# Three dead attention buffers as a landing zone for the next expert, copied to the ring by GpSimd

## The chip, the cores and the metric

One core of a Trainium2 chip runs the whole kernel. The time is device microseconds (us) of one execution, as the median of several runs. PE is TensorE, DVE is VectorE, ACT is ScalarE, POOL is GpSimd, SP is SyncE, whose only work here is to issue DMAs.

## What is computed

One transformer layer in float32 for 256 latent tokens of width 1024, with 256 context tokens: modulation rows from SiLU(c), neighbourhood attention over a 64-wide grid, a residual, and a mixture of 32 experts, four for each token.

```python
hx = modulate(x, norm_g[0], sh1, sc1)
mx = neighbourhood_attention(q, k, v, kc, vc, na_rpb) @ na_w_o
x = x + g1 * rms_norm(mx, norm_g[1])
hx2 = modulate(x, norm_g[2], sh2, sc2)
logits = hx2 @ w_router + b_router           # top 4 of 32, softmax over them: gates
for e in range(32):
    hid = hx2 @ w_up[e] + b_up[e]            # 1024 x 2048
    x_glu = minimum(hid[:, :1024], 7)
    x_lin = clip(hid[:, 1024:], -7, 7)
    act = x_glu * sigmoid(1.702 * x_glu) * (x_lin + 1)
    out = out + gates[:, e] * (act @ w_down[e] + b_down[e])    # 1024 x 1024
x = x + g2 * rms_norm(out, norm_g[3])
```

The weights of an expert are 12 MB (six chunks of 2 MB), those of all experts 403 million bytes. Each is read once.

## The kernel before

**Stages.** PE multiplies the modulation weights (`ada`), then the projections, then 16 rounds of attention (`DUOS`), the output projection (`wo`), the router, and then the blocks of experts. A block is up to 64 tokens of one expert (`SLOTS`). An expert with more than 64 tokens has two or more blocks; the tables that say which block belongs to which expert (`whose_i`, `ends_i`) are made on the chip in the first block, and `tables_ready` marks them.

**The ring.** All big weights go through `ring`, 12 places of 1 MB. In the expert stage it is six places of 2 MB, one for each chunk of an expert: chunks 0 to 3 are the up weights, 4 and 5 the down weights. So the ring holds one expert. SP loads chunk j of expert e when PE has used chunk j of the last block of expert e - 1: PE adds one to `ring_free` for each chunk of each block, SP waits for the count that the tables give, and the DMA adds to `expert_in[j]`. All these loads go through one DMA queue in the order of issue. PE waits for `expert_in[j]` ahead of chunk j (`expert_chunk_here`).

**One block on PE** (`block_step`), in the order of its queue: the up matmuls (L1201, 16 a chunk), the bias (L1211), `combine(0, b)` (L1187), transposes for the gates (L1223), the gather of the next block's tokens (L1127), `combine(1, b)` (L1187), which needs the accumulation of the first half (`acc_done`), the transposes of the activation (L1233, L1237), which need `act_ready`, the transposes of the next tokens (L1135), and the down matmuls (L1248).

**The same block on DVE**, in its queue: `glu` (L905) and `lin` (L906) from PSUM, `act = (lin + 1) * glu` (L909, both inputs in SBUF), `add_part(0)` (L899, twice, PSUM and SBUF), `act * sig` (L915, both inputs in SBUF, gives `act_ready`), `bsel` (L860), `aT` (L918), `add_part(1)` (L899), and the selection matrices for the next block (L854, L848). ACT makes the sigmoid (L579) and four copies out of PSUM.

**GpSimd** has done its last work ahead of the router (`powers(5, 1)`) and waits for `ms_ready` until the very end (`powers(6, 1)`).

**The memory** that matters: `kT_mem`, `tokens` (which also holds the attention bias) and `v_mem` are 2 MB each. After the attention `kT_mem` holds the residual `x1` and `h2T`, `tokens` the split biases of the experts (`bup_parts`, `bdown`), and `v_mem` the small tensors of the expert block (`xT`, `glu`, `lin`, `sig`, `act`, `aT`, `y`, `combT`). ACT issues the loads of `x1`, `b_up` and `b_down` when the attention ends; DVE splits `b_up` into three bfloat16 parts (`bup_split`) while PE is in the output projection.

Of the kernel before, what the change touches and what calls it, by code (L numbers as in the profile page):

```python
# [18 lines left out]
BF16 = mybir.dt.bfloat16  # L19
# [23 lines left out]
PER, UPS = 6, 4  # L43
# [3 lines left out]
def build(nc, x, c, ctx_in, c_ctx, ada_w, ada_b, norm_g, w_qkv, w_o, rpb, w_router, b_router,  # L47
          w_up, b_up, w_down, b_down, out):
    with ExitStack() as st:
# [9 lines left out]
        def sem(name):  # L59
# [8 lines left out]
        tokens = sb("tokens", [P, 4, D])  # L68
        bias = tokens[:, :, :].rearrange("p a d -> p (a d)")[:, 0:BIAS_SLOTS * BIAS_ROWS * GRID_W].rearrange(
            "p (b c) -> p b c", c=BIAS_ROWS * GRID_W)  # L70
# [6 lines left out]
        kT_mem = sb("kT_mem", [P, KC * 512])  # L77
        kT = kT_mem[:, :].rearrange("p (k t) -> p k t", k=KC)
        x1 = kT_mem[:, 0:2048].rearrange("p (t d) -> p t d", t=2)
        h2T = kT_mem[:, 2048:4096].rearrange("p (k t) -> p k t", k=KC)  # L80
# [3 lines left out]
        v_mem = sb("v_mem", [P, 4 * D])  # L84
        v = v_mem[:, :].rearrange("p (t d) -> p t d", t=4)

        xT = v_mem[:, 0:512].rearrange("p (j s) -> p j s", j=4)
        glu = v_mem[:, 512:1024]
        lin = v_mem[:, 1024:1536]
        sig = v_mem[:, 1536:2048]  # L90
        act = v_mem[:, 2048:2560]
        aT = v_mem[:, 2560:3072].rearrange("p (j s) -> p j s", j=4)
        y = v_mem[:, 3072:3584]
        combT = v_mem[:, 3584:3840].rearrange("p (t s) -> p t s", t=2)
        tmp = v_mem[:, 0:2048].rearrange("p (t d) -> p t d", t=2)
        junk = v_mem[:, 2048:3072]
# [4 lines left out]
        gate1, shift2, scale2, gate2 = mod  # L101

# [6 lines left out]
        adab = sb("adab", [P, 3, HALF])  # L109
        rows = sb("rows", [P, HALF])  # L110
# [34 lines left out]
        bup = tokens[0:E, 0:2, :].rearrange("p a d -> p (a d)")  # L145
        xe = hT_mem[:, 0:HALF]
        bup_parts = tokens[:, 2, :].bitcast(BF16)[0:3 * E, :]
        bup_part = hT_mem[0:E, 2048:3072].bitcast(BF16)
        bdown = tokens[0:E, 3, :]
# [8 lines left out]
        block_no = sb("block_no", [E, NCOL])  # L158
        whose_i = sb("whose_i", [1, NCOL], I32)
# [28 lines left out]
        wo_done, x1_ready, h2_ready = sem("wo_done"), sem("x1_ready"), sem("h2_ready")  # L188
        h2T_done, h2T_ready, logit_done = sem("h2T_done"), sem("h2T_ready"), sem("logit_done")
# [22 lines left out]
        def expert_chunk_here(eng, e, j):  # L212

            eng.wait_ge(expert_in[j], e * 16 + 16)
# [64 lines left out]
        def _(sp):  # L279
# [53 lines left out]
            def expert(e, blocks_before):  # L333
# [5 lines left out]
            for j in range(PER):  # L339
# [3 lines left out]
            with sp.Fori(1, E) as e:  # L343
                blocks_before = sp.value_load(ends_i[0:1, bass.ds(e - 1, 1)], min_val=1, max_val=E + MAX_EXTRA)
# [8 lines left out]
        def _(pool):  # L353
# [92 lines left out]
            for k in range(2, 6):  # L446
                powers(k, 1)
# [835 lines left out]
```

## Time and profile before

| | us |
|---|---|
| median of 3 runs | 1288.15 (1287.13 to 1288.61) |
| the profiled execution, its own time | 1288.93 |
| its span, first to last instruction | 1287.2 |
| PE busy | 1207.2 (94%) |
| DVE, ACT, POOL busy | 372.5, 185.8, 59.2 |
| chain that ended last: PE, DMA | 52%, 39% of the span |
| mean granted TensorE clock | 0.985 |

The span lacks 1.7 us of the execution's own time: what lies before the first and after the last instruction. The DMA engines moved 454 MB, 353 GB/s over the span. The stage of experts runs from 276.9 to the end and has 35 blocks (L905, which runs once a block, is counted 35 times): 32 experts, three of them with two blocks. A block in which nothing waits takes 27.3 us. "U" below is the time at which the first up matmul of a block starts.

### The profile page before, as it was taken

The numbers are of one execution on the slowest core, as the hardware profiler recorded it, in microseconds if no ns is written. First come the engines' busy times: TensorE is split into PE (matmuls) and PEld (weight loads), VectorE is DVE, ScalarE is ACT, GpSimd is POOL, SyncE is SP. The second block draws the span as 40 slices with busy tenths as digits, with TensorE's granted clock in tenths as the row PEclk, the third lists the DMA queues.
The fourth block names the chain that finished last, engine by engine and source line by source line (L and its number), as shares of the span: only waits on it lengthen the run. The fifth ranks groups of instructions, "written<-read, shape, count | busy, mean of one in ns | idle before, by whom it ended". The sixth has DMA issues, their size and how long they took to land.

```text
span 1287.2 us, 15187 instructions
## 1 busy us (share of the span) xinstructions
PE 1207.2 (94%) x5850; PEld 536.9 (42%) x5851; DVE 372.5 (29%) x737; ACT 185.8 (14%) x360; POOL 59.2 (5%) x89
## 2 busy tenths in 40 slices
PE   5899999889999999999999999999999999999996
PEld 1888655453343433333333333333443333333342
DVE  1944364631321112222111111122211122211114
ACT  2200264110111001110010000011110011101001
POOL 2230053000000000000000000000000000000000
PEclk9899999979999999999999999999999999999998
DMA  9973488309499999999999999999699999999590
GB/s 372 369 208 131 160 258 318 130 27 383 184 415 429 430 428 429 427 429 430 428 429 427 429 430 428 429 428 403 256 416 429 429 427 429 428 428 429 238 391 33
DMA packets 49044, 454.40 MB, mean 353 GB/s; under 512 B 16736, under 2 KB 16776, under 8 KB 20320
## 3 DMA queue, kind: packets, MB, share of 16 engines
q1 hardware_dynamic: 48064, 450.90, 84.7%
q0 software_dynamic: 512, 1.72, 0.4%
q10 hardware_dynamic: 448, 1.50, 0.4%
q8 instruction: 13, 0.21, 0.1%
q14 instruction: 7, 0.06, 0.0%
HBM read 453.06 MB, written 1.05 MB: 353 GB/s over the span
## 4 chain that ended last, share of the span: by engine, by line
PE 52%; DMA 39%; DVE 4%; issue 2%; ACT 1%; SPq 0%; POOL 0%; DVEq 0%; POOLq 0%
DMA ring<-in_moe_w_up 37%; PE pair L1201 23%; PE pair L1248 9%; PE pair L1010 9%; PE pair L1091 2%; DMA ring<-in_ada_w 2%; PE pair L1187 1%; PE pair L1026 1%; PE pair L968 1%; DVE hT_mem L899 1%; PE pair L1036 1%; PE pair L1049 1%; DVE v_mem L905 1%; DVE v_mem L906 1%; PE pair L1135 1%
## 5 line engine op out<-in xcount | busy, mean ns | idle before, releaser
L1201 PE MATMUL pair<-ring,v_mem 128*64 128x512 f32 x2240 | 495.8, 594 | 29.6 <-DMA ring<-in_moe_w_up 29.2
L1201 PEld LDWEIGHTS pair<-ring,v_mem 128*64 128x64 f32 x2240 | 181.1, 137 | 336.0 <-issue 274.5
L1248 PE MATMUL pair<-ring,v_mem 128*64 128x512 f32 x1120 | 248.1, 595 | 1.5
L905 DVE TENSOR_SCALAR v_mem<-pair 128x512 f32<-128x512 f32 x35 | 24.2, 692 | 719.8 <-PE pair L1211 719.8
L1248 PEld LDWEIGHTS pair<-ring,v_mem 128*64 128x64 f32 x1120 | 92.5, 137 | 132.9 <-issue 132.7
L579 ACT ACTIVATE v_mem<-v_mem 128x512 f32<-128x512 f32 x35 | 22.1, 630 | 538.8 <-DVE v_mem L905 538.8
L899 DVE TENSOR_TENSOR hT_mem<-hT_mem,pair 128x512 f32<-128x512 f32 x140 | 89.4, 680 | 8.0 <-PE pair L1187 8.0
L1187 PE MATMUL pair<-v_mem 64*128 64x512 f32 x280 | 78.8, 641 | 3.4 <-ACT v_mem L591 0.8
L1127 PE MATMUL pair<-q_mem,pT_mem 128*64 128x512 f32 x288 | 71.5, 618 | 1.3 <-DVE pT_mem L848 1.3
L379 POOL TENSOR_TENSOR rstd<-ms,neghalf 128x1 f32<-128x1 f32 (+1 forms) x8 | 4.7, 594 | 1071.7 <-DVE ms L627 1071.7
L591 ACT ACTIVATE v_mem<-pair 128x512 f32<-128x512 f32 x35 | 20.9, 597 | 228.7 <-PE pair L1248 228.7
L1010 PE MATMUL pair<-mod_high,ring_low 128*128 128x256 f32 (+1 forms) x128 | 44.7, 349 | 4.7 <-DVE ring_low L691 4.6
L1187 PEld LDWEIGHTS pair<-v_mem 64*128 64x128 f32 x280 | 21.2, 185 | 48.7 <-DVE hT_mem L899 32.6
L968 PE MATMUL pair<-ring,condT 128*32 128x512 f32 x192 | 25.7, 663 | 9.4 <-DMA ring<-in_ada_w 9.4
L564 ACT ACTIVATE hT_mem<-pair 128x512 f32<-128x512 f32 x36 | 21.5, 597 | 77.7 <-PE pair L1127 77.7
L1127 PEld LDWEIGHTS pair<-q_mem,pT_mem 128*64 128x64 f32 x288 | 17.8, 138 | 28.5 <-issue 27.1
L1010 PEld LDWEIGHTS pair<-mod_high,ring_low 128*128 128x128 f32 x128 | 25.4, 198 | 8.2 <-DVE ring_low L691 5.7
L1091 PE MATMUL pair<-ring,hT_mem 128*128 128x512 f32 x64 | 27.7, 594 | 0.0
L909 DVE SCALAR_TENSOR_TENSOR v_mem<-v_mem 128x512 f32<-128x512 f32 x35 | 24.2, 692 | 3.7
L918 DVE COPY v_mem<-pair 128x256 f32<-128x256 f32 x35 | 14.9, 424 | 35.1 <-PE pair L1233 35.1
L1010 PE MATMUL pair<-ring_low,mod_high 128*128 128x512 f32 x64 | 24.9, 389 | 0.0
L915 DVE TENSOR_TENSOR v_mem<-v_mem 128x512 f32<-128x512 f32 x35 | 24.0, 686 | 0.0
(217 smaller groups left out, 944.5 us busy)
## 6 DMA issues: line engine op xcount, KB each, us to landing
ring<-in_moe_w_up SPq DMA_DIRECT2D x128, 2048.0 KB, 23.2
ring<-in_moe_w_down SPq DMA_DIRECT2D x64, 2048.0 KB, 20.3
ring<-in_ada_w SPq DMA_DIRECT2D x24, 1024.0 KB, 8.4
ring<-in_na_w_qkv SPq DMA_DIRECT2D x12, 1024.0 KB, 27.4
ring<-in_na_w_o SPq DMA_DIRECT2D x4, 1024.0 KB, 15.1
tokens<-in_na_rpb SPq DMA_DIRECT2D x32, 96.0 KB, 6.4
gain<-in_norm_g POOLq DMA_DIRECT2D x3, 512.0 KB, 5.7
tokens<-in_x SPq DMA_DIRECT2D x1, 1024.0 KB, 5.0
```

What stands on the lines that cost most here:

```text
L579: s.activation(sig, glu, ACT.Sigmoid, scale=ALPHA).then_inc(sig_ready, 1)
L899: d.tensor_tensor(dst, dst, bank[banks[n]][:, :], ALU.add).then_inc(acc_done, 1)
L905: d.tensor_scalar(glu, bank[0][:, :], LIMIT, None, ALU.min).then_inc(glu_ready, 1)
L909: d.scalar_tensor_tensor(act, lin, 1.0, glu, ALU.add, ALU.mult).then_inc(pre_ready, 1)
L915: d.tensor_tensor(act, act, sig, ALU.mult).then_inc(act_ready, 1)
L968: last = mm(bank[b][32 * j:32 * j + 32, :], condT[:, k, :], wchunk(n)[:, HALF * j:HALF * j + HALF], start=k == 0, stop=k == KC - 1)
L1010: last = mm(out_, left, right, start=k == 0 and part == 0, stop=k == KC - 1 and part == 2)
L1091: last = mm(bank[4 + 2 * t + i][:, :], oT[:, k, P * t:P * t + P], wpair(WO, k)[:, HALF * i:HALF * i + HALF], start=k == 0, stop=k == KC - 1)
L1127: last = mm(bank[3][64 * n:64 * n + 64, :], pick[:, t, :], h2[:, t, HALF * n:HALF * n + HALF], start=t == 0, stop=t == 1)
L1187: mm(bank[banks[n]][:, :], combT[64 * n:64 * n + 64, t, :], y[64 * n:64 * n + 64, :], start=True, stop=True).then_inc(part_done, 1)
L1201: last = mm(bank[half][64 * n:64 * n + 64, :], xT[:, k % 4, 64 * (k // 4):64 * (k // 4) + 64], w[:, c0:c0 + HALF], start=k == 0, stop=False)
L1248: last = mm(bank[2][64 * n:64 * n + 64, :], aT[:, j, 64 * half:64 * half + 64], w[:, HALF * n:HALF * n + HALF], start=k == 0, stop=k == KC ...
```

## The change

The three 2 MB buffers become one tensor `zone`, and its three parts are the landing places of chunks 0, 1 and 2 of the next expert. SP loads them there (`staged_chunk`), and GpSimd copies each to its place in the ring (`g.tensor_copy`, 128 x 4096 float32) when the chunk has landed and the last block of the expert before has used that place. A tiny GpSimd operation on `home_mark` stands ahead of each copy. PE waits for the copy (`staged[j]`) in place of the landing for chunks 0 to 2. Chunks 3, 4 and 5 go straight to the ring as before.

The order of SP's queue becomes: chunks 0 to 3 of expert 0; chunks 0, 1, 2 of expert 1 into the zone as the attention gives its parts free (`s_done`, `bias_used`, `o_done`); chunks 4 and 5 of expert 0; then for each expert e from 1 on: chunks 3, 4, 5 of e, and behind them chunks 0, 1, 2 of e + 1 into the zone, each when the copy of the same chunk of e is done.

What was in the three buffers moves: the block's small tensors to `hT_mem` and two `mod` buffers (`glu` and `xe` share one place, `lin` and `act` another), `x1` to a buffer shared with `adab` and `rows`, `h2T` to `hT_mem`, the biases to `hT_mem`, `gain` and `mod[0]`. So the loads of `b_up` and `x1` are issued later, `b_down` behind the residual, `gate2` is made ahead of the split of `b_up`, ACT's squares wait for the split (`bup_split`), and `take_xe` waits for `pre_ready` and `sig_ready`.

```diff
-PER, UPS = 6, 4
+PER, UPS, STAGED = 6, 4, 3
+ZONE = 6
...
+        zone = sb("zone", [P, ZONE, 2048])
+        kT_mem = zone[:, 0:2, :].rearrange("p s n -> p (s n)")
+        token_mem = zone[:, 2:4, :].rearrange("p s n -> p (s n)")
+        v_mem = zone[:, 4:6, :].rearrange("p s n -> p (s n)")
...
+        v = v_mem.rearrange("p (t d) -> p t d", t=4)
+        tmp = acc
+        last_tmp = v_mem[:, 0:2048].rearrange("p (t d) -> p t d", t=2)
+        last_junk = v_mem[:, 2048:3072]
...
+        xT = hT_mem[:, 0:512].rearrange("p (j s) -> p j s", j=4)
+        glu, xe = hT_mem[:, 512:1024], hT_mem[:, 512:1024]
+        lin, act = hT_mem[:, 1024:1536], hT_mem[:, 1024:1536]
+        sig = hT_mem[:, 1536:2048]
+        aT = mod[2][:, 0:512].rearrange("p (j s) -> p j s", j=4)
+        y = mod[2][:, 512:1024]
+        combT = mod[1][:, 704:960].rearrange("p (t s) -> p t s", t=2)
...
+        row_mem = sb("row_mem", [P, 2 * D])
+        adab = row_mem[:, 0:3 * HALF].rearrange("p (g n) -> p g n", g=3)
+        rows = row_mem[:, 3 * HALF:4 * HALF]
+        x1 = row_mem[:, :].rearrange("p (t d) -> p t d", t=2)
...
+        junk = pT_mem[:, :]
+        bup = hT_mem[0:E, 2048:4096]
+        bup_parts = gain[:, :].bitcast(BF16)[0:3 * E, :]
+        bup_part = pT_mem[0:E, :].bitcast(BF16)
+        bdown = mod[0][0:E, :]
...
         def expert_chunk_here(eng, e, j):
-            eng.wait_ge(expert_in[j], e * 16 + 16)
+            if j < STAGED:
+                eng.wait_ge(staged[j], e + 1)
+            else:
+                eng.wait_ge(expert_in[j], e * 16 + 16)
+
+        def staged_chunk(j):
+
+            return zone[:, 2 * j:2 * j + 2, :].rearrange("p s n -> p (s n)")
...
-            def load_expert(e, j):
+            def load_expert(e, j, dst):
                 src = (up_2k[bass.ds(e, 1), j] if j < UPS else down_4k[bass.ds(e, 1), j - UPS])
-                sp.dma_start(expert_chunk(j), src.rearrange("a p n -> (a p) n")).then_inc(expert_in[j], 16)
-
...
+                sp.dma_start(dst, src.rearrange("a p n -> (a p) n")).then_inc(expert_in[j], 16)
+
+            for j in range(4):
+                sp.wait_ge(ring_free, EXP - RING + 2 * j + 2)
+                load_expert(0, j, expert_chunk(j))
+            sp.wait_ge(s_done, DUOS)
+            sp.wait_ge(expert_in[0], 16)
+            load_expert(1, 0, staged_chunk(0))
+            sp.wait_ge(bias_used, DUOS)
+            sp.wait_ge(expert_in[1], 16)
+            load_expert(1, 1, staged_chunk(1))
+            sp.wait_ge(o_done, DUOS)
+            sp.wait_ge(expert_in[2], 16)
+            load_expert(1, 2, staged_chunk(2))
+            for j in range(4, PER):
+                sp.wait_ge(ring_free, EXP - RING + 2 * j + 2)
+                load_expert(0, j, expert_chunk(j))
+
+            def second_half(e):
+
+                blocks_before = sp.value_load(ends_i[0:1, bass.ds(e - 1, 1)], min_val=1, max_val=E + MAX_EXTRA)
+                for j in range(STAGED, PER):
                     sp.wait_ge(ring_free, blocks_before * PER + (EXP - PER + j + 1))
-                    load_expert(e, j)
-
-            for j in range(PER):
-                sp.wait_ge(ring_free, EXP - RING + 2 * j + 2)
-                load_expert(0, j)
+                    load_expert(e, j, expert_chunk(j))
+
...
-                expert(e, blocks_before)
+            with sp.Fori(1, E - 1) as e:
+                second_half(e)
+                for j in range(STAGED):
+                    sp.wait_ge(staged[j], e + 1)
+                    load_expert(e + 1, j, staged_chunk(j))
+            second_half(E - 1)
             for t in range(2):
                 sp.wait_ge(fin_ready, t + 1)
-                sp.dma_start(out[0][P * t:P * t + P, :], tmp[:, t, :]).then_inc(out_done, 16)
+                sp.dma_start(out[0][P * t:P * t + P, :], last_tmp[:, t, :]).then_inc(out_done, 16)
...
+            for j in range(STAGED):
+                pool.wait_ge(expert_in[j], 16)
+                g.memset(staged_mark[:, j:j + 1], 0.0).then_inc(staged[j], 1)
+                g.memset(home_mark[:, j:j + 1], 0.0).then_inc(home_free[j], 1)
+            pool.wait_ge(tables_ready, 1)
+            with pool.Fori(1, E) as e:
+                blocks_before = pool.value_load(ends_i[0:1, bass.ds(e - 1, 1)], min_val=1, max_val=E + MAX_EXTRA)
+                for j in range(STAGED):
+                    pool.wait_ge(expert_in[j], e * 16 + 16)
+                    pool.wait_ge(staged[j], e)
+                    pool.wait_ge(home_free[j], e)
+                    pool.wait_ge(ring_free, blocks_before * PER + (EXP - PER + j + 1))
+                    mark = staged_mark[:, j:j + 1]
+                    g.tensor_tensor(home_mark[:, j:j + 1], mark, mark, ALU.add).then_inc(home_free[j], 1)
+                    g.tensor_copy(expert_chunk(j), staged_chunk(j)).then_inc(staged[j], 1)
...
-            sc.wait_ge(s_done, DUOS)
+            sc.wait_ge(o_done, DUOS)
+            sc.dma_start(bup, b_up[0]).then_inc(in_bup, 16)
+            sc.wait_ge(bc_done, 8)
             sc.dma_start(x1, token_rows(x)).then_inc(in_res, 16)
-            sc.wait_ge(bias_used, DUOS)
-            sc.dma_start(bup, b_up[0]).then_inc(in_bup, 16)
-            sc.dma_start(bdown, b_down[0]).then_inc(in_bdown, 16)
+            sc.wait_ge(bup_split, 1)
...
                 sc.wait_ge(x1_ready, t + 1)
+                if t == 1:
+                    sc.dma_start(bdown, b_down[0]).then_inc(in_bdown, 16)
                 sc.wait_ge(ssq_ready, 6 + 3 * t)
                 s.activation(junk, x1[:, t, :], ACT.Square, accum_out=ssq3[:, t:t + 1]).then_inc(ssq_ready, 1)
...
                 sc.wait_ge(gather_done, b + 1)
+                if not isinstance(b, int) or b > 0:
+                    sc.wait_ge(pre_ready, b)
+                    sc.wait_ge(sig_ready, b)
                 s.activation(xe, bank[3][:, :], ACT.Copy).then_inc(xe_ready, 1)
...
+            ve.wait_ge(in_gain, 48)
+            for i in range(2):
+                ve.wait_ge(bc_done, 6 + i + 1)
+                h = slice(HALF * i, HALF * i + HALF)
+                d.tensor_tensor(gate2[:, h], bank[2 + i][:, :], gain[:, h], ALU.mult).then_inc(bc_dve, 1)
+            ve.wait_ge(bc_dve, 6)
             ve.wait_ge(in_bup, 16)
...
             d.tensor_copy(bup_parts[2 * E:3 * E, :], bup).then_inc(bup_split, 1)
-            ve.wait_ge(in_gain, 48)
-            for i in range(2):
-                ve.wait_ge(bc_done, 6 + i + 1)
-                h = slice(HALF * i, HALF * i + HALF)
-                d.tensor_tensor(gate2[:, h], bank[2 + i][:, :], gain[:, h], ALU.mult).then_inc(bc_dve, 1)
...
-                d.tensor_tensor(tmp[:, t, :], acc[:, t, :], gate2[:, :], ALU.mult).then_inc(gated, 1)
+                d.tensor_tensor(last_tmp[:, t, :], acc[:, t, :], gate2[:, :], ALU.mult).then_inc(gated, 1)
```

## Rows read from the trace of the kernel before

**Rows 1.** The page, second part: busy tenths of the 16 DMA engines in 40 slices of 32.2 us.

```profile
DMA  9973488309499999999999999999699999999590
```

**Rows 2.** Chain that ended last, in order of time: start us, us, what.

```profile
471.36 13.75 PE pair L1201 x64
...
509.76 3.68 PE pair L1201 x16
513.59 25.48 DMA ring<-in_moe_w_up
539.12 3.68 PE pair L1201 x16
...
891.50 3.65 PE pair L1201 x16
...
1045.21 13.75 PE pair L1201 x64
...
1201.06 3.65 PE pair L1201 x16
```

**Rows 3.** The chain and the timeline of one block, 334.87 to 362.17: start us, us.

```profile
334.87 13.73 PE pair L1201 x64
...
362.17 13.73 PE pair L1201 x64
...
350.47 0.69 DVE L909 SCALAR_TENSOR_TENSOR v_mem<-v_mem 128x512 f32<-128x512 f32 x1
...
351.08 1.28 DVE L899 TENSOR_TENSOR hT_mem<-hT_mem,pair 128x512 f32<-128x512 f32 x2
...
352.27 0.69 DVE L915 TENSOR_TENSOR v_mem<-v_mem 128x512 f32<-128x512 f32 x1
...
353.47 0.51 PE L1233 MATMUL pair<-ident,v_mem 128*128 128x128 f32 x2
```

**Rows 4.** Timeline of SP's issues of expert loads: start us, us, count.

```profile
304.31 3.77 SPq L331 DMA_DIRECT2D ring<-in_moe_w_down  x2
...
338.48 10.63 SPq L331 DMA_DIRECT2D ring<-in_moe_w_up  x4
...
358.90 3.77 SPq L331 DMA_DIRECT2D ring<-in_moe_w_down  x2
...
912.33 10.63 SPq L331 DMA_DIRECT2D ring<-in_moe_w_up  x4
```

**Rows 5.** DMA issues begun in 338 to 340, and in 365 to 367: KB, us to landing.

```profile
ring<-in_moe_w_up SPq DMA_DIRECT2D x1, 2048.0 KB, 7.6
...
ring<-in_moe_w_up SPq DMA_DIRECT2D x1, 2048.0 KB, 11.8
```

**Rows 6.** GpSimd groups by line: busy us, mean ns of one, idle before.

```profile
L440 POOL TENSOR_SCALAR mod<-mod,rinv 128x512 f32<-128x512 f32 x32 | 21.7, 691 | 38.1 <-DVE rinv L749 38.1
L429 POOL TENSOR_TENSOR tokens<-tokens,wmask 128x384 f32<-128x384 f32 x16 | 18.3, 1145 | 12.0 <-DMA tokens<-in_na_rpb 12.0
...
L400 POOL TENSOR_SCALAR qcol<-qcol 128x1 f32<-128x1 f32 x1 | 0.2, 234 | 0.1
```

**Rows 7.** Timeline of GpSimd and of VectorE, 55 to 64.

```profile
55.37 1.67 POOL L413 TENSOR_TENSOR hT_low<-hT_mem,mod_high 128x512 fp32r<-128x512 f32 x1 [1.50 <-DVE mod_high L678]
...
55.93 2.20 DVE L691 TENSOR_TENSOR ring_low<-ring,pT_high 128x1024 fp32r<-128x1024 f32 x1
...
62.08 1.23 DVE L691 TENSOR_TENSOR ring_low<-ring,pT_high 128x1024 fp32r<-128x1024 f32 x1
```

**Rows 8.** PE timeline with the gap before; a stretch: length, five busy times, PEclk.

```profile
21.59 1.43 PE L968 MATMUL pair<-ring,condT 128*32 128x512 f32 x8 [2.95 <-DMA ring<-in_ada_w]
...
22.50:23.00 0.50, 0.50 (x5) 0.05 (x1) 0.50 (x2) 0.00 (x0) 0.50 (x1) 0.50 0.87 361
```

**Rows 9.** Timeline of ACT's issue before the router, and of DVE in the first block.

```profile
221.34 0.44 ACTq L534 DMA_DIRECT2D tokens<-in_moe_b_down  x1
...
294.67 0.69 DVE L909 SCALAR_TENSOR_TENSOR v_mem<-v_mem 128x512 f32<-128x512 f32 x1
```

More of the change, by code:

```diff
@@ L67, in build @@
         ring = sb("ring", [P, RING, 2048])
-        tokens = sb("tokens", [P, 4, D])
-        bias = tokens[:, :, :].rearrange("p a d -> p (a d)")[:, 0:BIAS_SLOTS * BIAS_ROWS * GRID_W].rearrange(
-            "p (b c) -> p b c", c=BIAS_ROWS * GRID_W)
+        zone = sb("zone", [P, ZONE, 2048])
+        kT_mem = zone[:, 0:2, :].rearrange("p s n -> p (s n)")
+        token_mem = zone[:, 2:4, :].rearrange("p s n -> p (s n)")
+        v_mem = zone[:, 4:6, :].rearrange("p s n -> p (s n)")
+        tokens = token_mem.rearrange("p (a d) -> p a d", d=D)
+        bias = token_mem[:, 0:BIAS_SLOTS * BIAS_ROWS * GRID_W].rearrange("p (b c) -> p b c", c=BIAS_ROWS * GRID_W)
         hT_low_mem = also("hT_low", [P, KC * 512])
@@ L76, in build @@
         acc = hT_mem[:, 2048:4096].rearrange("p (t d) -> p t d", t=2)
[L77 to L80, printed above, removed]
+        kT = kT_mem.rearrange("p (k t) -> p k t", k=KC)
+        h2T = hT_mem[:, 0:2048].rearrange("p (k t) -> p k t", k=KC)
         q_mem = sb("q_mem", [P, KC * TOK])
@@ L144, in build @@
         br = sb("br", [P, E])
[L145 to L149, printed above, removed]
+        junk = pT_mem[:, :]
[3 more added lines that the diff above has]
+        bdown = mod[0][0:E, :]
         rank_e, gate_e2 = small[:, 0:2, :], small[:, 4:6, :]
@@ L158, in build @@
         block_no = sb("block_no", [E, NCOL])
+        staged_mark = sb("staged_mark", [1, STAGED])
+        home_mark = sb("home_mark", [1, STAGED])
         whose_i = sb("whose_i", [1, NCOL], I32)
@@ L188, in build @@
         wo_done, x1_ready, h2_ready = sem("wo_done"), sem("x1_ready"), sem("h2_ready")
+        staged = [sem(f"staged{j}") for j in range(STAGED)]
+        home_free = [sem(f"home_free{j}") for j in range(STAGED)]
         h2T_done, h2T_ready, logit_done = sem("h2T_done"), sem("h2T_ready"), sem("logit_done")
@@ L336, in expert @@
+            for j in range(4, PER):
[4 more added lines that the diff above has]
+                for j in range(STAGED, PER):
                     sp.wait_ge(ring_free, blocks_before * PER + (EXP - PER + j + 1))
-                    load_expert(e, j)
-            for j in range(PER):
-                sp.wait_ge(ring_free, EXP - RING + 2 * j + 2)
-                load_expert(0, j)
+                    load_expert(e, j, expert_chunk(j))
@@ L342, in _ @@
             sp.wait_ge(tables_ready, 1)
-            with sp.Fori(1, E) as e:
-                blocks_before = sp.value_load(ends_i[0:1, bass.ds(e - 1, 1)], min_val=1, max_val=E + MAX_EXTRA)
-                expert(e, blocks_before)
+            with sp.Fori(1, E - 1) as e:
[4 more added lines that the diff above has]
+            second_half(E - 1)
             for t in range(2):
@@ L600, in _ @@
                 sc.wait_ge(ssq_ready, 10 + t)
-                s.activation(junk, acc[:, t, :], ACT.Square,
+                s.activation(last_junk, acc[:, t, :], ACT.Square,
                              accum_out=ssq4[:, t:t + 1]).then_inc(ssq_ready, 1)
@@ L936, in _ @@
                 ve.wait_ge(rstd_ready, 7 + t)
-                d.scalar_tensor_tensor(tmp[:, t, :], tmp[:, t, :], rstd[:, 6 + t, 0:1], x1[:, t, :],
+                d.scalar_tensor_tensor(last_tmp[:, t, :], last_tmp[:, t, :], rstd[:, 6 + t, 0:1], x1[:, t, :],
                                        ALU.mult, ALU.add).then_inc(fin_ready, 1)
```

15 lines of the change are left out of this document (removed).

## The prediction

> **What bounds the kernel now.** I read the page first. Its busy shares name PE, but the 16 DMA engines [rows 1] stand at nine tenths or more from slice 12 on, save in slices 29 and 38 (6 and 5 tenths), and at 4 in slice 11. So no share decides: the two take turns. The chain in order of time [rows 2] shows the turns. Five blocks end with an up stage of 13.75 us without a wait (the last starts at 471.36); then each block waits 25.5 us for a landing and does only its last chunk (16 matmuls) behind it. Those ends are 29.36 us apart (509.76, 539.12): the time in which the queue moves six chunks, 4.89 us each. PE alone needs 27.30 us a block [rows 3], so it loses 2.06 us a block here. The first such stretch has 14 blocks, 485 to 895: without waits its last up stage would end at 471.36 + 14 x 27.30 + 13.73 = 867.3, and it ends at 891.50 + 3.65 = 895.15, 27.9 us lost. The second has five: 1045.21 + 5 x 27.30 + 13.73 = 1195.4 against 1204.7, 9.3 us. Together **37.1 us**, all that better supply could give in this stage.
>
> What separates the stretches are the three experts with two blocks. SP's issues [rows 4] show the first: after 304.31 nothing is issued until 338.48, for the ring is full and its places come free only in the second block (U = 334.87). The others end at 912.33 and near 1222. After each the queue is empty.
>
> **Does the zone bring supply?** In a block without waits SP issues chunk 4 at U - 3.3, chunk 5 at U, the next chunks 0 to 3 at U + 3.6 to U + 13.9 [rows 3, 4]. In the full queue only order counts, and the order of chunks is the same after the change: 3, 4, 5 of an expert, then 0, 1, 2 of the next, since SP puts the zone loads behind chunk 5. Three chunks land earlier during a double block, but chunk 3 still waits for the last use of its place, as before, so the queue runs dry there again, and the stream that sets the next stretch starts with chunk 4 at the same place (U - 3.3) as before. I see no gain. The five early chunks of the start are lost the same way: the first double is expert 1.
>
> **The copy's own price.** No row has a GpSimd copy. One-input TENSOR_SCALAR takes 0.234 us for one element a partition and 0.691 for 512 [rows 6]: 0.894 ns an element, 3.9 us for 4096. A plain copy has no scalar to read; I take 3.8. Bounds: eight times the 512 row, 5.5; the rate of the two-input row L429 (1.145 us for 384), 12.2. Below, no row excludes less. The operation on `home_mark` is 0.25 by the one-element row. Where PE waits for the stream, it now restarts at the copy of chunk 2: that landing is 4.89 earlier than that of chunk 3, plus 0.25 + 3.8 + 0.1, plus two chunks of 3.43, against 3.65 for the one chunk: 6.1 - 3.65 = 2.5 us later, paid once in each of the two stretches: 5 us, if nothing else happens.
>
> The Trainium skill (GPSIMD Engine Reference, Performance versus the Vector engine) gives 1.8 cycles an element as best case, 769 ns for 512; the row here has 691 ns and disagrees. By the page's rate the copy would be 6.1 us, an estimate, and the sum that of the last rival.
>
> **The hold.** DVE's L691 (two SBUF inputs) takes 1.23 us alone, and 2.20 when GpSimd's L413 is running: it starts at 55.93, L413 ends at 57.04, and 57.04 + 1.1 is just its end [rows 7]. So DVE waits for the whole of the other's instruction; of two that wait I let the earlier go first, GpSimd too. In the block, DVE has two operations with both inputs in SBUF, L909 and L915, and both are on PE's path [rows 3]. L413 has two inputs, the copy one; the rows can't show whether the copy holds DVE too. I take it that it does.
>
> That is the rule of the Trainium skill too (SBUF — State Buffer, Who interferes with whom): the pair of ports is an exclusive lock for the whole instruction, between any GpSimd instruction that reads SBUF and a DVE one with two SBUF inputs. It speaks against this change; for two inputs the trace agrees.
>
> **Where the copies fall, one block of a one-block expert.** A chunk issued into an empty queue lands after 7.6 us [rows 5]. Chunk 4, issued at U - 3.3, lands at U + 4.3, chunk 5 at 9.2, and the next expert's chunks 0, 1, 2 at 14.1, 19.0, 23.9 (before: chunk 0 at 365.8 + 11.8, U + 15.4, with some queue left over [rows 5]). Their places are long free.
> - Copy 0 runs from 14.35 to 18.15. L909 is due at 15.6 (350.47 [rows 3], where U + 13.73 = 348.60 ends the up stage). It waits until 18.15.
> - L909 and the two L899 take 1.8: L915 is due at 19.95. Copy 1 has been there since 19.25 and holds until 23.05. L915 ends at 23.7.
> - L1233 started at U + 18.6, 0.5 after L915 could let it. It now starts at 23.75: **5.15 us later**, and all behind it on PE's queue: the down matmuls, the block's end, and through `ring_free` SP's next chunk 4.
> - Copy 2 (24.15 to 27.95) holds only DVE's selection matrices, due one block later.
> The block takes 32.45 us. That is over 29.36, so the queue has run empty when the next chunk 4 is issued, and the next block repeats it. Nothing pulls it back.
>
> How many: the copies for expert e + 1 run in the last block of e. Experts 2 to 19 give 18 such blocks, 21 to 29 give 9. In the second block of experts 1, 20 and 30 the chunks have landed long before, and the copies run from U + 3.7 to 15.7, ahead of L909. 27 x 5.15 = **+139.0**. The DMA waits vanish, since a period of 32.4 is over the queue's: **-37.1**. In the first block the copies start at 288 and sit on L909 (294.67 [rows 9]) and L915: L915 ends 3.2 later, of which 2 was spare: **+1.2**.
>
> **The rest.** ACT issues the load of `b_down` between the residual and the square that the router waits for: **+0.4**, by the issue of 0.44 [rows 9]. The later loads of `b_up` and `x1` and the split lie under the output projection (27.7 us); by my count the DVE queue is through 0.7 us before the last half is due, so a late `gain` costs up to 2 us. This goes to the range. New waits in `take_xe` end when L909 does, ahead of the gather's end; moved tensors have the same shapes: 0. What the tail loses: GpSimd has left its loop a block before.
>
> Sum: 139.0 - 37.1 + 1.2 + 0.4 = +103.5 on the profiled execution's 1288.93: 1392.4. That execution is 0.8 over the median 1288.15, so I predict **1392 us**; for this case alone 1380 to 1410 (copy 3.4 to 4.5 us).
>
> **Rivals.**
> - *The clock falls too.* PE has two idle stretches a block, 2.4 and 2.7 us, with 1.1 us of work between. Before, PE fell to 1.2 GHz after a gap of 2.95 us (PEclk 0.50 [rows 8]). If 3 us of each down stage run at half speed, 1.5 us a block: +40, 1432 us. For it: the gap is nearly as long; against: each is shorter.
> - *One hold at most.* If the copy takes under 3.1 us, L915 comes before copy 1. The hold on L909 alone brings the block to about 29.36, the DMA's rate: 27 x 2.06 - 37.1 + 1.6 = +20, 1308 us.
> - *No hold.* A one-input copy doesn't stop DVE. Then 5.0 + 0.4: 1294 us. For it: no row shows it.
> - *The slow copy.* From 4.65 us the copies queue behind each other; at 5.5, L915 ends at 26.6, 8 us late a block: +180, 1470 us and more.
> - *The other side: the lead holds.* If three staged chunks did put the queue ahead, 3 x 4.89 = 14.7 us less in the first stretch and all 9.3 in the second: -24, 1265 us. It decides when zone loads start before the queue would be empty anyway; SP's order, behind chunk 5, speaks against it.
>
> **Chances.** Two holds 0.46, with the clock 0.14, one hold 0.13, no hold 0.12, slow copy 0.08, the lead 0.04, no difference 0.03. The range runs from no hold (1293) to the clock case with some more (1450); outside lie the lead, no difference, the slow copy and a deeper fall of the clock, 0.2. A measurement of this kernel tells 0.2% (2.6 us) from no change; faster 0.04, within it 0.03, slower 0.93.
>
> **What would show it.** GpSimd's copy row with 93 copies of near 3.8 us; L909 and L915 with means well over 0.69 us; blocks 32.4 us apart from expert 2 on, without waits for DMA; doubles' second blocks at 27.3; the DMA slices near nine tenths throughout. Wrong, if L915 keeps 0.69 while a copy runs (no hold), if blocks are 29.36 apart (one hold), or if PEclk falls in the blocks.

## The result, and the profile after

| kernel | us, median | runs | from to | profiled: own time, span | TensorE clock |
|---|---|---|---|---|---|
| before, on the same chip | 1287.64 | 4 | 1287.08 to 1288.61 | | 0.985 |
| after | 1450.49 | 4 | 1449.58 to 1452.45 | 1452.45, 1450.7 | 0.917 |

The ratio is 1.127 (95% interval 1.1246 to 1.1285): slower by 163 us, where I had forecast 1392 us, and half a microsecond above the range's end. The direction and the main mechanism, two holds in each of 27 blocks, are the forecast ones. The size is 58 us off, for the most part because the forecast had no term for the TensorE clock.

In the kernel after, line numbers are higher: the up matmul L1201 is L1253, the down matmul L1248 is L1300, DVE's L909 and L915 are L961 and L967, the transposes L1233 are L1285. From the page of the kernel after, second part (granted clock, busy DMA engines, in 40 slices of 36.3 us), then groups:

```profile
PEclk9999999689988889999999999999999999999999
DMA  9863687135888888888888888888388888888831
...
L493 POOL COPY ring<-zone 128x4096 f32<-128x4096 f32 x93 | 333.7, 3588 | 0.0
L957 DVE TENSOR_SCALAR hT_mem<-pair 128x512 f32<-128x512 f32 x35 | 24.2, 692 | 681.8 <-PE pair L1263 681.8
L1300 PE MATMUL pair<-ring,mod 128*64 128x512 f32 x1120 | 291.2, 679 | 0.3
...
L492 POOL TENSOR_TENSOR home_mark<-staged_mark 1x1 f32<-1x1 f32 x93 | 17.2, 185 | 787.0 <-DMA zone<-in_moe_w_up 634.1
...
L967 DVE TENSOR_TENSOR hT_mem<-hT_mem 128x512 f32<-128x512 f32 x35 | 107.4, 3067 | 0.0
L961 DVE SCALAR_TENSOR_TENSOR hT_mem<-hT_mem 128x512 f32<-128x512 f32 x35 | 93.0, 2657 | 3.7
```

A copy takes 3.59 us (3.8 taken), its mark 0.18. L961 and L967, 0.69 us each before [rows 3], now have means of 2.7 and 3.1; L957, which reads PSUM, stays at 0.69. The DMA slices, nine tenths before [rows 1], are at eight. TensorE's waits in the kernel after (us in total, times, longest) show where that goes:

```profile
PE pair L1285 <- DVE hT_mem L967: 69.4, 27, 2.6
PE pair L1239 <- DVE hT_mem L951: 66.9, 27, 2.7
```

27 of each, in the 27 blocks that were counted, and no wait for an expert load is left: the 37.1 us of before are gone, and 136.3 us (5.05 a block) stand in their place. One such block starts at 377.71 and the next at 412.07. The timeline of the kernel after, for this block on GpSimd, DVE and TensorE, then for the first block on GpSimd and DVE (start us, us, and in brackets the idle time before):

```profile
392.11 3.59 POOL L493 COPY ring<-zone 128x4096 f32<-128x4096 f32 x1
...
397.02 3.59 POOL L493 COPY ring<-zone 128x4096 f32<-128x4096 f32 x1
...
393.31 2.94 DVE L961 SCALAR_TENSOR_TENSOR hT_mem<-hT_mem 128x512 f32<-128x512 f32 x1
...
397.37 3.79 DVE L967 TENSOR_TENSOR hT_mem<-hT_mem 128x512 f32<-128x512 f32 x1
...
397.50 1.13 PE L1239 MATMUL pair<-mod 64*128 64x512 f32 x4 [2.33 <-DVE hT_mem L951]
401.22 0.70 PE L1285 MATMUL pair<-ident,hT_mem 128*128 128x128 f32 x2 [2.59 <-DVE hT_mem L967]
...
299.21 3.59 POOL L493 COPY ring<-zone 128x4096 f32<-128x4096 f32 x1
302.77 0.18 POOL L492 TENSOR_TENSOR home_mark<-staged_mark 1x1 f32<-1x1 f32 x1
302.90 3.59 POOL L493 COPY ring<-zone 128x4096 f32<-128x4096 f32 x1
...
302.27 4.76 DVE L961 SCALAR_TENSOR_TENSOR hT_mem<-hT_mem 128x512 f32<-128x512 f32 x1
```

The first copy ends at 395.70, and L961 is through 0.55 later (396.25); the second ends at 400.61, and L967 is through at 401.16. Two holds, two gaps, 4.92 us. But the block is 34.36 long and the block without waits 27.30 [rows 3], so 2.1 us are missing. They are in the granted clock of TensorE. Stretches of the same kernel (length, then the five engines' busy times, PEclk, DMA share, GB/s):

```profile
398.00:400.00 2.00, 0.63 (x4) 0.00 (x0) 2.00 (x1) 0.39 (x1) 2.00 (x1) 1.00 1.01 434
400.00:402.00 2.00, 0.78 (x4) 0.79 (x5) 1.31 (x3) 0.00 (x0) 0.83 (x3) 0.52 1.00 426
402.00:404.00 2.00, 2.00 (x8) 1.09 (x8) 2.00 (x4) 0.98 (x2) 2.00 (x1) 0.50 1.01 434
404.00:406.00 2.00, 2.00 (x8) 0.71 (x6) 2.00 (x4) 0.00 (x0) 1.50 (x1) 0.50 0.73 311
406.00:408.00 2.00, 2.00 (x8) 0.52 (x6) 0.17 (x2) 0.00 (x0) 0.00 (x0) 0.77 0.00 0
```

After the two gaps the clock stands at 0.50 (1.2 GHz) from about 400 to 407, the down stage takes 8.87 us instead of 7.09 (8.4 to 8.7 in the later ones of the 27), and its group's mean is 679 ns where it was 595. The last row also shows the queue empty (DMA share 0.00), as forecast: the next chunk waits for the late down stage.

Two terms more are at the start. TensorE's first up matmul is at 284.55 instead of 276.94. From DVE's waits in the kernel after:

```profile
DVE mod L833 <- DMA gain<-in_norm_g: 13.6, 1, 13.6
```

GpSimd issued this load of 512 KB at 226.33, and it landed 13.2 us later, at 239.57; in the kernel before it took 3.9. SP had issued three zone loads of 2 MB, at 214.17, 214.90 and 223.63; the first had just landed, and the other two (landing at 233.79 and 240.88) were on the way at the same time. `gate2` and the split of `b_up`, which DVE's queue holds ahead of the router's work, wait with it.

The first block takes 38.57 us instead of 30.64. Here the three copies run back to back (last four timeline lines). L961 has been waiting since 302.27, the copy ends at 302.80, the next starts at 302.90, and L961 is through at 307.03, after that one too: of two that wait, the earlier did not go first. TensorE stands for 3.40 us there, and its clock is at 0.50 for 10.2 us from 307.9 on.

The account of the span, +163.5 (1450.7 - 1287.2): start +7.6, first block +7.9, the waits for DMA -37.1, and the rest, 185.1, over 27 blocks is 6.86 a block. The block starts give the same: 615.01 us for 18 blocks and 307.24 for 9 are 34.16 each, 6.86 over 27.30. Of it 5.05 are gaps (136.3 / 27) and 1.8 is work at half clock.

### The profile page after: what moved, and what is told of

Its sections match the earlier page's. It is cut to its first block, busy times and chain, and to the rows that moved or that the text cites. A ratio compares the mean times of both kernels' runs of the same rounds, so it can differ in the third digit from the quotient of the medians.

```text
span 1450.7 us, 15779 instructions
## 1 busy us (share of the span) xinstructions
PE 1262.2 (87%) x5850; PEld 532.7 (37%) x5851; DVE 573.2 (40%) x737; ACT 185.7 (13%) x360; POOL 404.7 (28%) x282
## 4 chain that ended last, share of the span: by engine, by line
PE 72%; DVE 15%; issue 8%; DMA 3%; ACT 1%; POOL 0%; SPq 0%; DVEq 0%; POOLq 0%; ACTq 0%
PE pair L1253 33%; PE pair L1300 20%; PE pair L1062 7%; DVE hT_mem L967 7%; DVE hT_mem L951 2%; PE pair L1187 2%; DMA ring<-in_ada_w 2%; DVE hT_mem L957 2%; DVE hT_mem L958 1%; PE pair L1285 1%; PE pair L1263 1%; PE pair L1078 1%; PE pair L1289 1%; PE pair L1020 1%; PE pair L1088 1%
## 5 line engine op out<-in xcount | busy, mean ns | idle before, releaser
L1253 PE MATMUL pair<-ring,hT_mem 128*64 128x512 f32 x2240 | 487.0, 592 | 0.2 <-issue 0.2
L493 POOL COPY ring<-zone 128x4096 f32<-128x4096 f32 x93 | 333.7, 3588 | 0.0
L957 DVE TENSOR_SCALAR hT_mem<-pair 128x512 f32<-128x512 f32 x35 | 24.2, 692 | 681.8 <-PE pair L1263 681.8
L1300 PE MATMUL pair<-ring,mod 128*64 128x512 f32 x1120 | 291.2, 679 | 0.3
L1253 PEld LDWEIGHTS pair<-ring,hT_mem 128*64 128x64 f32 x2240 | 163.8, 137 | 315.9 <-issue 315.9
L1300 PEld LDWEIGHTS pair<-ring,mod 128*64 128x64 f32 x1120 | 90.2, 158 | 181.0 <-issue 181.0
L1239 PE MATMUL pair<-mod 64*128 64x512 f32 x280 | 78.8, 640 | 68.2 <-DVE hT_mem L951 66.9
L967 DVE TENSOR_TENSOR hT_mem<-hT_mem 128x512 f32<-128x512 f32 x35 | 107.4, 3067 | 0.0
L961 DVE SCALAR_TENSOR_TENSOR hT_mem<-hT_mem 128x512 f32<-128x512 f32 x35 | 93.0, 2657 | 3.7
L1285 PE MATMUL pair<-ident,hT_mem 128*128 128x128 f32 x70 | 23.2, 430 | 69.4 <-DVE hT_mem L967 69.4
L906 DVE TENSOR_SCALAR pT_mem<-slot_no,rank_col,gate_col 128x128 f32<-128x128 f32 x70 | 68.3, 1016 | 0.0
L1285 PEld LDWEIGHTS pair<-ident,hT_mem 128*128 128x128 f32 x70 | 11.1, 208 | 98.5 <-DVE hT_mem L967 97.0
L1187 PE MATMUL pair<-ident,hT_mem 128*128 128x128 f32 x144 | 35.3, 393 | 0.0
```

Source lines behind the costliest of these rows:

```text
L493: g.tensor_copy(expert_chunk(j), staged_chunk(j)).then_inc(staged[j], 1)
L906: ins = d.tensor_scalar(comb[:, t, :, :], slot_no[:, :, :], ranks[:, t, bass.ds(b, 1)], gates[:, t, bass.ds(b, 1)], ALU.is_equal, ALU.mult)
L957: d.tensor_scalar(glu, bank[0][:, :], LIMIT, None, ALU.min).then_inc(glu_ready, 1)
L961: d.scalar_tensor_tensor(act, lin, 1.0, glu, ALU.add, ALU.mult).then_inc(pre_ready, 1)
L967: d.tensor_tensor(act, act, sig, ALU.mult).then_inc(act_ready, 1)
L1187: last = tr(bank[3][:, P * j:P * j + P], xe[:, c0:c0 + 2 * P - 1:2], ident[:, :])
```

## The experiments

Times are medians; the kernel before, run on the same chips, gave 1287.2 to 1287.4 us. All are edits of the kernel after.

**1. The copies where DVE has nothing left to do.** In GpSimd's loop, ahead of each copy:

```diff
                     pool.wait_ge(ring_free, blocks_before * PER + (EXP - PER + j + 1))
+                    pool.wait_ge(act_ready, blocks_before)
```

> Each copy also waits until DVE has finished act * sig of that block (act_ready), so no copy can stand in front of the two operations with both inputs in SBUF. Theory (the holds and the clock that falls after them are the loss inside the blocks): the 27 long blocks go back to 27.3 us where the DMA allows it, PEclk stays at 1.00, the DMA-bound stretches return, and the time is 1288 + 7.6 (late start of the experts) + 5 (chunk 2 goes over a copy, twice) = about 1301 us. Rival (the moved small tensors make the block slow): still 1430 or more. Rival (the wait for landing and copy of chunk 2 is the loss): no change, 1450.

1297.19 us (4 runs), ratio 1.008 [1.0063, 1.0093]. The same 93 copies of 3.59 us move the same bytes; 153 us of the 163 are gone. DVE's two operations and TensorE's waits in its profile:

```profile
L962 DVE SCALAR_TENSOR_TENSOR hT_mem<-hT_mem 128x512 f32<-128x512 f32 x35 | 24.2, 693 | 3.7
...
L968 DVE TENSOR_TENSOR hT_mem<-hT_mem 128x512 f32<-128x512 f32 x35 | 23.9, 683 | 0.0
```

```profile
PE pair L1254 <- POOL ring L494: 31.0, 38, 1.2
```

So the holds, with the clock that falls behind them, are the cause, and not the copies' traffic. What TensorE waits for now is a copy that itself waited for its load: in the chain those waits stand 29.37 us apart, the queue's period as in [rows 2]. The staged chunks bring nothing even without holds: 9.8 us over before, of which 4.7 is the late start (first up matmul at 281.6). The prediction priced the two restarts behind a copy at 2.5 us each. The traces give the two stretches 2.3 and 2.1 us more than that of experiment 2, which has the same layout without copies, but only 1.4 and 1.3 more than that of the kernel before (spans 1294.6 and 1287.2, 7.4 apart); so this term is known no better than that.

**2. Only the moved tensors.** No zone loads and no copies; all the rest of the change stays.

```diff
-            for j in range(4):
+            for j in range(PER):
                 sp.wait_ge(ring_free, EXP - RING + 2 * j + 2)
                 load_expert(0, j, expert_chunk(j))
...
+            sp.wait_ge(tables_ready, 1)
+            with sp.Fori(1, E) as e:
                 blocks_before = sp.value_load(ends_i[0:1, bass.ds(e - 1, 1)], min_val=1, max_val=E + MAX_EXTRA)
-                for j in range(STAGED, PER):
+                for j in range(PER):
                     sp.wait_ge(ring_free, blocks_before * PER + (EXP - PER + j + 1))
                     load_expert(e, j, expert_chunk(j))
...
-            for j in range(STAGED):
-                pool.wait_ge(expert_in[j], 16)
...
```

> The changed kernel with all its moved tensors, new waits and reordered ACT and DVE queues, but without landing zone and copies: SP loads all six chunks straight to the ring as before the change. Theory (all of the loss comes from the copies and from the early zone loads): 1288 to 1290 us, at most 2 over the kernel before. Rival (the new places and waits cost in every block): 35 blocks times 1 us or more, 1325 and up.

1288.08 us (11 runs), ratio 1.001 [0.9997, 1.0015]: no difference. The new order in DVE's and ACT's queues costs nothing by itself, and the first up matmul is at 275.9: the late start needs the zone loads.

**3. The small loads first.** SP waits until `gain`, the residual and `b_up` have landed before it issues the first zone load:

```diff
+            sp.wait_ge(in_gain, 48)
+            sp.wait_ge(in_res, 16)
+            sp.wait_ge(in_bup, 16)
             sp.wait_ge(s_done, DUOS)
             sp.wait_ge(expert_in[0], 16)
             load_expert(1, 0, staged_chunk(0))
```

> The changed kernel, but SP issues the first three zone loads only when gain, b_up and x1 have landed. Theory (the 7.6 us by which the first expert block starts late come from those small loads queueing behind 6 MB of zone loads): gain lands in 4 to 6 us in place of 13, the first up matmul starts near 277 in place of 284.6, and the time is 1450.5 - 7.5 = 1443 us. Rival (the order of DVE's queue, gate2 ahead of the split, is the cause): 1449 to 1451.

1442.30 us (4 runs), ratio 1.121 [1.1191, 1.1226]: 8.2 us of the 163 are the late start. The load of `gain` lands after 5.3 us, and the first up matmul is at 277.2. With experiment 1's edit as well:

> Copies wait for act * sig, and the first zone loads wait for gain, b_up and x1: both losses taken away, the copy on the way of chunk 2 left. Theory: the experts start within 1 us of the kernel before and each of the two DMA-bound stretches ends 2.5 us later: 1287.4 + 5 + 0.5 = 1293 us. If staging brought any lead into the stretches, it would show here as less than 1288; if the late start has another cause, 1297 as without the second edit.

1291.14 us (6 runs), ratio 1.003 [1.0021, 1.0045]: what is left of the change, with its two costs out of the way, is 4 us slower than before (some 2 by the profiled spans).

**4. Short holds.** Each copy in eight pieces of 512 elements, so that DVE could get in between two:

```diff
-                    g.tensor_copy(expert_chunk(j), staged_chunk(j)).then_inc(staged[j], 1)
+                    for i in range(8):
+                        q = slice(HALF * i, HALF * i + HALF)
+                        ins = g.tensor_copy(expert_chunk(j)[:, q], staged_chunk(j)[:, q])
+                    ins.then_inc(staged[j], 1)
```

> The changed kernel with each copy cut into eight GpSimd copies of 128 x 512. Theory A (a hold lasts as long as one GpSimd instruction, and a waiting DVE operation goes next): no hold over 0.6 us, at most 1 us more a block, blocks at the DMA's 29.36, clock at 1.00: 1288 + 7.6 + 10 to 20, 1305 to 1315 us. Theory B (pieces that follow each other without a gap keep DVE out until the last, as the copies back to back did in the first block, where the operation due at 302.27 waited past one copy's end at 302.8 for the next one's at 306.5): no better than the whole copies, 1440 to 1480 us. Rival (DVE's waits have another cause than the copy): 1450 too, but with DVE's operations long where no piece runs.

1578.93 us (4 runs), ratio 1.227 [1.2249, 1.2286]: outside what either theory gave; the 27 blocks stand 38.7 us apart. A block of its timeline on GpSimd and DVE, and TensorE's waits:

```profile
431.70 4.50 POOL L495 COPY ring<-zone 128x512 f32<-128x512 f32 x8
...
436.74 4.50 POOL L495 COPY ring<-zone 128x512 f32<-128x512 f32 x8
...
441.77 4.49 POOL L495 COPY ring<-zone 128x512 f32<-128x512 f32 x8
...
432.91 3.83 DVE L964 SCALAR_TENSOR_TENSOR hT_mem<-hT_mem 128x512 f32<-128x512 f32 x1
...
437.87 3.91 DVE L970 TENSOR_TENSOR hT_mem<-hT_mem 128x512 f32<-128x512 f32 x1
441.70 4.61 DVE L915 CAST mod<-mod 96x64 bf16 x1
```

```profile
PE pair L1242 <- DVE hT_mem L954: 95.9, 30, 3.8
PE pair L1303 <- DVE mod L973: 77.8, 27, 2.9
PE pair L1288 <- DVE hT_mem L970: 63.1, 27, 2.7
```

The eight pieces follow each other without a gap and take 4.50 us. L964 waits since 432.91 through all that are left and is through at 436.74, 0.54 after the eighth; the cast at 441.70, issued before the first piece, is through only at 446.31. So pieces back to back are one hold, 0.9 us longer than the whole copy, and the third copy now reaches a third operation, the cast of 96x64. Behind the cast sits L973, which writes the half of `aT` that the down stage waits for. Where the mark stands between the second copy and the third, L970 does get its turn: it is through at 441.78 and the mark takes 0.47 us instead of 0.18 for that, in all 27 blocks.

**5. The copies after the first of the two operations only.**

```diff
+                    pool.wait_ge(pre_ready, blocks_before)
```

> Each copy waits until DVE has finished act = (lin + 1) * glu (pre_ready), so it can no longer hold that one, but still stands in front of act * sig. Theory: one gap of about 2 us in PE's queue in place of two (2.3 and 2.6), the clock stays at 1.00, the blocks take 29.4 us, near the DMA's own 29.36, and the time is 1288 + 7.6 + 27 x 2.06 - 37 + 3 = about 1317 us. Rival (any gap over 2 us makes the clock fall): 27 x 3.8 - 37 + 8, about 1360 us. If the moved tensors were the cause: 1450.

1467.37 us (4 runs), ratio 1.140 [1.1383, 1.1418]. All that was expected missed: one hold less was aimed at, and it is slower than the change itself. Its timeline on GpSimd, DVE and TensorE shows that the number of holds did not fall:

```profile
464.47 3.59 POOL L494 COPY ring<-zone 128x4096 f32<-128x4096 f32 x1
468.02 0.63 POOL L493 TENSOR_TENSOR home_mark<-staged_mark 1x1 f32<-1x1 f32 x1
468.60 3.59 POOL L494 COPY ring<-zone 128x4096 f32<-128x4096 f32 x1
...
463.50 0.69 DVE L962 SCALAR_TENSOR_TENSOR hT_mem<-hT_mem 128x512 f32<-128x512 f32 x1
...
465.30 3.30 DVE L968 TENSOR_TENSOR hT_mem<-hT_mem 128x512 f32<-128x512 f32 x1
468.53 3.71 DVE L913 CAST mod<-mod 96x64 bf16 x1
472.16 0.41 DVE L971 COPY mod<-pair 128x256 f32<-128x256 f32 x1
...
468.66 0.51 PE L1286 MATMUL pair<-ident,hT_mem 128*128 128x128 f32 x2 [2.09 <-DVE hT_mem L968]
...
472.62 5.55 PE L1301 MATMUL pair<-ring,mod 128*64 128x512 f32 x14 [2.73 <-DVE mod L971]
```

L962 isn't held any more, but the first copy now holds L968, and the second holds the cast of `bsel`, which I had not counted: it has one input, 96x64, takes 0.18 us alone, and waits 3.5 us all the same. L971, next in DVE's queue, releases the down stage. The gaps are 2.1 and 2.7 us, and the down stage behind them runs at half clock (PEclk 0.50 at 472 to 476), so that a block takes 34.1 us, as in the change. There are 31 such gaps of each kind and not 27, since copies that wait for `pre_ready` fall on DVE's work in the second blocks of the three double experts too: three more blocks at 6.8 us, which with an earlier first up matmul (281.8) and a shorter first block make the 15 us between the two profiled spans. Here DVE did get its turn between two copies: L968 ends at 468.60, and the mark waits for it (0.63 instead of 0.18), all 31 times.

The first block of this kernel has a gap of 2.7 us with only a short one ahead of it:

```profile
304.70 0.51 PE L1286 MATMUL pair<-ident,hT_mem 128*128 128x128 f32 x2 [0.54 <-DVE hT_mem L968]
...
308.67 9.47 PE L1301 MATMUL pair<-ring,mod 128*64 128x512 f32 x32 [2.74 <-DVE mod L971]
```

PEclk is 0.67 in 306 to 308 and 0.50 in 308 to 312 there, and the down stage takes 9.47 us instead of 7.09. So it doesn't take two gaps of over 2 us.

**6. The clock by itself.** Eight more matmuls a block (`fill(4)` twice; 256 columns each, into half of a bank that is free then), four ahead of the second combination and four ahead of the wait for `act`. Nothing that they compute is used.

```diff
+                    fill(4)
                     combine(1, b)
 
+                fill(4)
                 pe.wait_ge(act_ready, b + 1)
```

> The changed kernel with four spare matmuls (256 columns, into an unused part of a bank) ahead of combine(1) and four ahead of the wait for act * sig, some 0.9 us each, so PE's two gaps of 2.3 and 2.6 us shrink to 1.4 and 1.7; the output is untouched. Theory (gaps near 2.5 us let the clock fall and cost about 1.9 us in each of 27 blocks, beside 4.9 us of hold): PEclk stays at 1.00, the 27 blocks go from 34.1 to 32.3, the 8 others lose 1.8 each: 1450.5 - 49 + 14 = about 1415 us. Rival (the clock has no part; the down matmuls are slow for another reason, as their operands' new places): 1450 + 14 = 1465 us.

1413.61 us (4 runs), ratio 1.098 [1.0965, 1.0999]: 36.9 us less than the change. DVE and GpSimd do what they did. Stretches of its profile over the two holds of a block:

```profile
404.00:406.00 2.00, 2.00 (x11) 1.44 (x8) 2.00 (x1) 0.38 (x1) 2.00 (x1) 1.00 1.03 442
406.00:408.00 2.00, 1.36 (x10) 0.97 (x8) 1.50 (x4) 0.18 (x1) 0.83 (x3) 1.00 0.98 418
408.00:410.00 2.00, 1.96 (x11) 0.81 (x11) 2.00 (x3) 0.80 (x2) 2.00 (x1) 1.00 1.03 442
```

The clock stays at 1.00, the down stage is back at 7.09 us, and the block takes 32.0 us (up stages at 383.16 and 415.19), near the 32.45 that the prediction has for holds alone. So the holds and the clock are two terms, as the account says. The gaps that remain (0.58 and 0.64 us) are not the whole hold, since the fill takes its place. The 36.9 us are a balance: the 27 blocks take 31.9 instead of 34.2, some 60 us less, and the seven blocks behind the first one that have no gap take 30.4 instead of 27.3, 22 us more.

**7. The same memory without the copy.** The buffers stay dead, but nothing is moved in them: nine places of 2 MB (six of the ring, three of the zone) in three groups, and the halves of each expert go through the groups in turn. Each chunk is loaded when the chunk nine before it has been used. TensorE's code of a block is written out three times, once for each turn; the core of the edit:

```diff
+        def expert_place(r, j):
+
+            where, first = ((ring, 6), (ring, 0), (zone, 0))[(2 * r + j // 3) % 3]
+            s = first + 2 * ((j + 2) % 3)
+            return where[:, s:s + 2, :].rearrange("p s n -> p (s n)")
...
+            def half(e, r, js, shift):
+
+                blocks_before = blocks_until(sp, e - (2 if shift > 0 else 1))
+                for j in js:
+                    sp.wait_ge(ring_free, blocks_before * PER + (EXP - PER + j + shift + 1))
+                    load_expert(e, j, r)
...
+            with pe.Fori(0, (E - 2) // 3) as turn:
+                for i in range(1, 4):
+                    expert_blocks(turn * 3 + i, turn + i // 3, i % 3)
```

Experiment 3's three waits are in it as well, and `expert_blocks` loops over the blocks of one expert.

> Nine places of 2 MB and no copy: the three places in the dead buffers join the six of the ring, an expert's three-chunk halves go through the three groups of places in turn, TensorE's code of a block is written out once for each of the three turns, and each chunk is loaded as soon as the chunk nine before it has been used. The three small loads (gain, residual, b_up) land before the first load into the dead buffers, as in the run with that order. Theory A (the loads set the pace: blocks stand 29.37 us apart there, while TensorE alone needs 27.3 us for one, and what can be won is the queue's idle time while an expert's second block needs no load): three chunks more in store, 3 x 4.9 = 14.7 us of loading, can be carried out of the first double expert and out of the twentieth, at most 29.4 us; counted through chunk by chunk with those two periods about 23 us less than before, 1264 us, and 1258 to 1272 as bounds. Rival B (depth isn't the limit, or the longer code of TensorE and SyncE costs what it brings): 1285 to 1295 us. Rival C (every load that lands earlier meets something that is slower for it, as with the copies): over 1300 us.

1265.21 us (5 runs), ratio **0.983** [0.9816, 0.9842]: 22 us less than the kernel before. The page's DMA slices, TensorE's waits for expert loads, and the chain in order of time of this kernel:

```profile
DMA  9974387828399999999999999999999999999840
```

```profile
PE pair L1227 <- DMA ring<-in_moe_w_up: 6.5, 8, 1.2
...
PE pair L1227 <- DMA zone<-in_moe_w_up: 4.0, 5, 1.2
```

```profile
334.89 13.73 PE pair L1227 x64
...
362.18 13.73 PE pair L1227 x64
...
666.04 34.66 DMA zone<-in_moe_w_up
...
894.15 13.73 PE pair L1227 x64
...
1221.70 13.73 PE pair L1227 x64
```

The queue keeps nine tenths through the first two doubles (slice 29 of before [rows 1] has no counterpart) and until the loads run out in slices 38 and 39. Blocks follow at 27.30 us until after the up stage of 662.43, then the queue sets the pace for some eight blocks: 894.15 - 662.43 - 8 x 27.30 = 13.3 us lost where it was 27.9 [rows 2], and nothing in the second stretch where it was 9.3. That is 23.9 us, the whole difference of the two profiled spans (1287.2 - 1263.3). The code of TensorE and SyncE that is written out three times cost nothing that shows: blocks still follow at 27.30. The first up matmul is at 276.96.

## Why the prediction was right and wrong

- **The step that failed.** The sum has no term for the clock behind the two gaps: the prediction left it to a rival, and gave as the reason that "each is shorter". It cost 49 us. The late start (7.6) and the first block (7.9 where 1.2 was taken) add 14; holds that were 3 us cheaper take some back. That gives the 60 us between the 103.5 of the sum and the 163.5 of the spans.
- **No supply: right.** The three staged chunks brought nothing even where neither holds nor the late start were in the way (second run of experiment 3, 1291.14 us). SP's order behind chunk 5 was the reason given; the chain of experiment 1, at the queue's period again, fits it, and no run changes that order alone. Experiment 7 shows it from the other side: with all nine places in one order the lead is there, and it was worth what the rival *the lead holds* had priced at 24 (22 by the medians).
- **The copy holds DVE: right.** It was an assumption, since no row shown of before had a one-input GpSimd operation beside DVE's; the means of 2.7 and 3.1 us after, and of 0.69 and 0.68 in experiment 1, show it. By the rule of the Trainium skill (SBUF — State Buffer, Who interferes with whom) any GpSimd instruction that reads SBUF does this; the trace agrees. The same section names DVE's casts and copies from SBUF in their two-port modes as well, which I had left out: experiment 5's cast, with 3.7 us, agrees with that too.
- **Two holds in 27 blocks, doubles free: right.** 27 waits of each kind; the second blocks of the double experts take 27.3 us. The gaps are 5.05 us a block (4.92 in the block shown) against 5.15, with a copy of 3.59 and a mark of 0.18, where I took 3.8 and 0.25: 136 instead of 139. The prediction gives the Trainium skill's rate for GpSimd as another price and calls the sum by it that of the last rival; it is that of *the slow copy*, the last but one, and the copy is not slow.
- **The DMA waits vanish, -37.1: right.**
- **The clock: the term that was mis-sized, at zero.** I put it among the rivals (1.5 us a block, chance 0.14) and said against it that "each is shorter" than the gap of 2.95 us of [rows 8]. They are shorter, 2.33 and 2.59, and that was no reason: the clock fell to 0.50 all the same, for 6.8 us in each of the 27 blocks, and a gap of 2.74 with one of 0.54 ahead of it did it in experiment 5. It cost 1.8 us a block, 49 us; experiment 6, which held the clock at 1.00, won back 37 net of what its fill costs where there is no gap. This is most of the 58 us.
- **The late start: mis-sized.** I gave a late `gain` up to 2 us and put it in the range. I had followed DVE's queue, but not the load itself: it shared the DMA engines with two zone loads of 2 MB and the residual. 7.6 us in the profiled execution; experiment 3 gained 8.2.
- **The first block: +7.9 instead of +1.2.** What failed here is "of two that wait I let the earlier go first". With copies back to back L961 was passed over for a whole copy (302.27), which it was in the first blocks of experiment 3's first run and of experiment 6 too (4.76 and 4.75 us), and the down stage behind it ran at half clock (9.08 us).

With the measured terms the sum is 7.6 + 7.9 - 37.1 + 27 x 6.86 = 163.6 against the 163.5 of the spans. That the result lies only half a microsecond outside the range is chance: the range was drawn for other reasons, and three misses of one sign add up to the difference. What stays open is who goes next when both wait. Between the pieces of a copy in experiment 4 DVE never went. Where a mark stands between two copies, the `tensor_tensor` went first each time (experiments 4 and 5), and the `scalar_tensor_tensor` of the first block was passed over each time (after a wait of 2.3 us too, in experiment 4); no run here changes the operation alone, so that this decides it isn't shown. Of the clock, the granted share falls at 400.1 in the block shown, within the second gap; a gap of 2.74 us almost alone was followed by the fall, one of 1.67 alone (experiment 4, at 368.88) was not, and no run has one of 2.3 to 2.6 alone.

## What to carry to other kernels

A GpSimd copy between two places in SBUF is not free because GpSimd is idle: look for every DVE operation with operands in SBUF, casts too, that falls within it and lies on another engine's path. Behind the first of them the copy only held the next (experiment 5); behind the last one on the path it held nothing that counts (experiment 1). Cutting the copy into pieces that follow each other doesn't help. Where memory comes free, add it to the ring by its addresses instead of staging into it. Where a hold gives TensorE gaps of 2 to 3 us, the stage behind them is to be priced at half clock too; and a large early load is to be checked against every small load of the other queues that is issued while it is on its way.

## What the runs showed of the hardware

- A GpSimd copy of 128x4096 floats from SBUF to SBUF takes 3588 ns, 0.88 ns an element; eight of 128x512 take 4.50 us back to back. The Trainium skill (GPSIMD Engine Reference, Performance versus the Vector engine) gives 1.8 cycles an element as best case, and in the sentence before it 1.03 cycles for short bodies. With the 1.2 GHz of its example these are 1.5 and 0.86 ns, an estimate; the copy's 0.88 agrees with the second.
- While it runs, DVE's operations with two SBUF inputs wait, and so does a cast of one SBUF input (96x64 to bf16, 0.18 us alone, 3.7 in experiment 5) and a `tensor_scalar` of 128x128 with one tensor input (L906, twice a block, 0.34 us each before; in the 27 blocks the first of the two, under the third copy, took 2.1); L957, with its input in PSUM, keeps 0.69.
- Eight GpSimd instructions back to back kept DVE out for all of them (3.83 and 3.91 us).
- With gaps of 2.33 and 2.59 us and 1.13 us of matmuls between, TensorE's granted clock was 0.50 for 6.8 us, from within the second gap on. With the gaps cut to about 0.6 us each it stayed at 1.00. A gap of 2.74 us with one of 0.54 ahead of it brought 0.50 too.
- A load of 512 KB on GpSimd's queue landed after 13.2 us with two of 2 MB on SP's and one of 1 MB on ACT's under way, and after 5.3 (experiment 3) and 3.9 (before) without those on SP's.
